# First phase of an encoder layer: summed rows, order of the next piece's sums, block-wise input turning, wider cumulation products

## The chip, the core and the metric

The kernel runs on one core of a Trainium2 chip. The metric is the device time of one execution in microseconds (us). Engines that appear below: TensorE (PE, with its weight loads PEld), VectorE (DVE), ScalarE (ACT), GpSimd (POOL) and SyncE (SP); POOL, SP and ACT issue DMA transfers.

## The reference

One layer of a hybrid encoder on x of 512 tokens by 2048, float32. A modulation vector made from the conditioning vector c shifts and scales the normalised input; one projection feeds attention (8 query heads, 2 key and value heads) and a gated delta net (8 heads, forward and backward), then come the output projection and a gated MLP.

```python
mod = silu(c) @ w_ada[l] + b_ada[l]              # 2048 x 12288
sh1, sc1, gt1, sh2, sc2, gt2 = jnp.split(mod, 6, axis=-1)
hn = rms_norm(h) * (1.0 + sc1) + sh1             # 512 x 2048
proj = hn @ w_in[l]
...
gc = jnp.cumsum(g.reshape(B, H, N, C), axis=-1)  # running sums of the log decay
```

The first phase of the kernel computes sh1, sc1 and hn, and the projections of both key and value heads of the attention, the first key and query heads of the delta net, and the 32 gate columns (ba).

## The kernel before

**Matrix products.** A float32 weight tile is split by ScalarE into w_hi (split, line 546, the copy in 551) and by VectorE into w_lo = raw - w_hi (low, 908, line 911); the activation is held as act_hi and act_lo. Three products (hi*hi, hi*lo, lo*hi; lines 1453 to 1455 in the first phase, 1359 to 1361 later) give one 128 x 128 x 512 step. A unit is eight weight tiles of 128 x 128 in one of two slots raw[0], raw[1]; SP loads unit u after lo_made counts u - 1.

**The first phase** runs over PIECES = (0,4), (4,8), (8,12), (12,14), (14,16): column tiles of 128 of the 2048 features. For piece j the modulation columns (shift and scale, 2 x 128 x the piece's width) are a sum over 16 row blocks k of w_ada. POOL loads all of them in order of j and k (line 491), into five slots for summed rows (DD, EG, CL, T, act) and two for turned rows (ka, va); it waits, in this order, until a slot's last reader is done.
- Summed rows: VectorE multiplies the block by cond[:, k] and adds it to an accumulator (first_add, 913, lines 924 and 927); accumulators alternate between ada_acc and PTb. Twelve of 16.
- Turned rows, TURNED_ROWS = (3, 7, 11, 15): TensorE multiplies the block by the column cond[:, k] (first_turned, 1416, line 1423), straight into the sum in PSUM.
- first_sums(j) (1408, line 1412) adds the accumulator's partitions on TensorE, first_columns(j) (929, lines 934 and 935, VectorE) adds the bias and writes mod, ScalarE writes act_hi and hn_tmp for each feature tile (lines 598 and 602), VectorE writes act_lo (normed, 953, line 957).
- TensorE multiplies the piece by the weights of three units (first_unit, 1442): units 3j to 3j+2 for full pieces; units 9 and 10 for (12,14), 10 and 11 for (14,16). ba_part (1459, line 1464) makes the gate columns.

The order of the work is written out by hand on each engine. TensorE, for a full piece:

```python
                for i in range(3):
                    first_unit(3 * j + i, k0, k1)
                    first_turned(j + 1, TURNED_ROWS[i])
                if j:
                    ba_part(*PIECES[j - 1])
                first_turned(j + 1, TURNED_ROWS[3])
                first_sums(j + 1)
```

VectorE runs all 12 summed rows of a piece, with the lows of the current units between them, then first_columns and normed, and only then the next piece's rows.

**Before the first piece** x (four blocks of 128 tokens, one DMA each, all counted on one semaphore) is squared, normalised by ScalarE (lines 576 to 584), turned by TensorE in 16 feature tiles of four blocks (line 1437) and copied to x_feat by ScalarE (line 590). TensorE starts on that behind all four turned rows of piece 0; ahead of these it turns the vector rows (line 1395) into col, once all small transfers have landed.

**After the phase** the weights of head 0 are multiplied (early, 1505) while the gates are worked out: 16 products of 8 columns make running sums within a block of 128 tokens (line 1527). The level masks are loaded as float32, cast by VectorE to bfloat16 (line 1027), and head 0 starts behind that cast.

## Time and profile before

| | us |
|---|---|
| median of 3 runs | 2695.82 |
| lowest, highest | 2693.03, 2696.62 |
| profiled execution | 2691.72 |
| its span | 2689.9 |

In the profiled execution PE is busy for 96% of the span, DVE for 52%, ACT for 38%, POOL for 8%. In 40 equal slices of the span (digits are tenths) the first two or three stand out:

```profile
PE   4889999999999989988999999999999999999997
DVE  3645666666666666445444444444444444444454
...
PEclk9889999999999989999999999999999999999998
DMA  8752544544544525432333333333333333333233
```

A slice is 67.2 us. PEclk is the granted clock of TensorE in tenths of full speed; DMA is the mean busy share of 16 transfer engines.

### The profile page before, as it was taken

The page shows a single profiled execution, that of the slowest core. Times are in us where ns is not written, and L with a number is a line of the kernel's source. Part 1 is how long each engine was busy: PE and PEld are TensorE (multiplying, and loading weights), DVE is VectorE, ACT ScalarE, POOL GpSimd, SP SyncE. Part 2 cuts the span into 40 slices and gives each one's busy share as a digit, 9 for nine tenths or more (in the row PEclk, how much of TensorE's full clock was granted, in tenths as well). Part 3 has the DMA queues.
Part 4 walks back from the last instruction along what each step waited for, and adds up shares of the span by engine and source line. Part 5 has one row for each costly group of instructions (what it writes and reads, how often), then busy time and mean ns, then how long its engine had stood idle before and what let it go on. Part 6 is the DMA issues. An engine that isn't in the chain of part 4 may idle for free.

```text
span 2689.9 us, 35982 instructions
## 1 busy us (share of the span) xinstructions
PE 2587.1 (96%) x12454; PEld 2126.7 (79%) x12454; DVE 1408.2 (52%) x1830; ACT 1029.2 (38%) x1438; POOL 214.2 (8%) x286
## 2 busy tenths in 40 slices
PE   4889999999999989988999999999999999999997
PEld 4777887888888868866888888888888888888885
DVE  3645666666666666445444444444444444444454
ACT  5224354354354353334443234442244432223334
POOL 2320211211211212100000000000000000000000
PEclk9889999999999989999999999999999999999998
DMA  8752544544544525432333333333333333333233
GB/s 290 274 171 68 154 123 125 156 120 129 151 118 131 152 86 153 139 88 71 94 95 91 96 101 100 94 92 96 101 94 100 94 88 96 104 101 94 87 92 126
DMA packets 431809, 318.46 MB, mean 118 GB/s; under 512 B 12902, under 2 KB 403857, under 8 KB 431249
## 3 DMA queue, kind: packets, MB, share of 16 engines
q1 hardware_dynamic: 401648, 212.19, 27.3%
q0 software_dynamic: 29184, 104.87, 12.1%
q10 hardware_dynamic: 929, 0.74, 0.1%
q8 instruction: 33, 0.54, 0.1%
q14 instruction: 15, 0.12, 0.0%
HBM read 313.56 MB, written 4.19 MB: 118 GB/s over the span
## 4 chain that ended last, share of the span: by engine, by line
PE 92%; DVE 3%; DMA 2%; ACT 1%; issue 1%; DVEq 0%; ACTq 0%; POOL 0%; POOLq 0%
PE pw L1359 23%; PE pw L1361 22%; PE pw L1360 22%; PE pw L1343 2%; PE pw L1345 2%; PE pw L1344 2%; PE pd L1626 2%; PE pd L1649 1%; PE pd L1662 1%; PE pd L1609 1%; DMA EG<-in_w_ada_dram 1%; PE pd L1669 1%; PE pd L1423 1%; DMA va<-in_w_ada_dram 1%; PE pd L1453 1%
## 5 line engine op out<-in xcount | busy, mean ns | idle before, releaser
L1359 PE MATMUL pw<-act_hi,w_hi 128*128 128x512 f32 x2016 | 813.5, 404 | 14.9 <-DVE act_lo L1254 8.7
L911 DVE TENSOR_TENSOR w_lo<-raw,w_hi 128x1024 fp32r<-128x1024 f32 x426 | 520.9, 1223 | 527.0 <-ACT w_hi L551 524.5
L1361 PE MATMUL pw<-act_hi,w_lo 128*128 128x512 f32 x2016 | 787.9, 391 | 0.0
L1360 PE MATMUL pw<-act_lo,w_hi 128*128 128x512 f32 x2016 | 786.2, 390 | 0.0
L551 ACT ACTIVATE w_hi<-raw 128x1024 fp32r<-128x1024 f32 x426 | 450.1, 1057 | 525.9 <-PE pw L1361 411.8
L1359 PEld LDWEIGHTS pw<-act_hi,w_hi 128*128 128x128 f32 x2016 | 379.6, 188 | 108.1 <-issue 24.9
L1361 PEld LDWEIGHTS pw<-act_hi,w_lo 128*128 128x128 f32 x2016 | 379.3, 188 | 81.5
L1360 PEld LDWEIGHTS pw<-act_lo,w_hi 128*128 128x128 f32 x2016 | 380.1, 189 | 80.4 <-issue 6.9
L1359 PE MATMUL pw<-mh_hi,w_hi 128*128 128x512 f32 x704 | 276.1, 392 | 1.6 <-DVE w_lo L911 1.6
L1361 PE MATMUL pw<-mh_hi,w_lo 128*128 128x512 f32 x704 | 274.2, 389 | 0.0
L1360 PE MATMUL pw<-mh_lo,w_hi 128*128 128x512 f32 x704 | 274.0, 389 | 0.0
L1279 DVE TENSOR_SCALAR cv<-gp,col 128x512 f32<-128x512 f32 x88 | 48.1, 547 | 298.4 <-ACT gp L847 298.4
L847 ACT ACTIVATE gp<-pw 128x512 f32<-128x512 f32 x88 | 52.7, 599 | 339.0 <-PE pw L1361 339.0
L1359 PEld LDWEIGHTS pw<-mh_hi,w_hi 128*128 128x128 f32 x704 | 132.2, 188 | 31.3 <-DVE w_lo L911 2.5
L946 DVE SCALAR_TENSOR_TENSOR ada_acc<-ada_w,cond,ada_acc 128x1024 f32<-128x1024 f32 x120 | 153.6, 1280 | 5.4 <-DMA ada_w<-in_w_ada_dram 3.8
L1361 PEld LDWEIGHTS pw<-mh_hi,w_lo 128*128 128x128 f32 x704 | 132.1, 188 | 27.8
L1360 PEld LDWEIGHTS pw<-mh_lo,w_hi 128*128 128x128 f32 x704 | 132.2, 188 | 26.9
L1283 DVE SCALAR_TENSOR_TENSOR cv<-gp,col,cv 128x512 f32<-128x512 f32 x176 | 132.4, 752 | 26.0 <-DVE cv L1283 5.2
L1343 PE MATMUL pw<-act_hi,w_hi 128*128 128x512 f32 x256 | 104.1, 407 | 10.0 <-DVE act_lo L1036 8.1
L1127 DVE SCALAR_TENSOR_TENSOR T<-pd,cst_sb,T 128x256 f32<-128x256 f32 x96 | 42.0, 480 | 127.7 <-PE pd L1662 127.7
L500 POOL DMA_DIRECT2D ada_w<-in_w_ada_dram x128 | 71.3, 557 | 411.1 <-DVE ada_acc L946 402.1
L1345 PE MATMUL pw<-act_hi,w_lo 128*128 128x512 f32 x256 | 100.5, 393 | 0.0
(280 smaller groups left out, 2682.4 us busy)
## 6 DMA issues: line engine op xcount, KB each, us to landing
raw<-in_w_up_dram SPq DMA_DIRECT2D x176, 512.0 KB, 3.9
ada_w<-in_w_ada_dram POOLq DMA_DIRECT2D x128, 512.0 KB, 4.4
raw<-in_w_in_dram SPq DMA_DIRECT2D x84, 512.0 KB, 3.9
raw<-in_w_down_dram SPq DMA_DIRECT2D x64, 384.0 KB, 3.4
raw<-in_w_down_dram SPq DMA_DIRECT2D x64, 320.0 KB, 3.1
raw<-in_w_out_dram SPq DMA_DIRECT2D x32, 512.0 KB, 4.4
DD<-in_w_ada_dram POOLq DMA_DIRECT2D x8, 512.0 KB, 8.2
mixed<-in_x_dram SPq DMA_DIRECT2D x4, 1024.0 KB, 13.4
```

The lines of the kernel that those rows point to most:

```text
L500: pool.dma_start(ada_w[k % 2][:], A["w_ada"][0, k * P:(k + 1) * P, bass.ds((4 + h) * ADA_W, ADA_W)]) \
L551: nc.scalar.activation(w_hi[slot][:], raw[slot][:], ACT.Copy).then_inc(hi_made.sem, 1)
L911: V.tensor_tensor(w_lo[slot][:], raw[slot][:], w_hi[slot][:].bitcast(F32), ALU.subtract).then_inc(lo_made.sem, 1)
L946: V.scalar_tensor_tensor(ada_acc[:], w, cond[:, k:k + 1], ada_acc[:], ALU.mult, ALU.add).then_inc(ada_step.sem, 1)
L1283: V.scalar_tensor_tensor(cv[:, part, :], gp[:, part, j:j + S], w[j], cv[:, part, :], ALU.mult, ALU.add) \
L1343: M(pw[slot][:], w_hi[slot][:, k, :], act_hi[:, t, :], start=k == 0, stop=False)
L1344: M(pw[slot][:], w_hi[slot][:, k, :], act_lo[:, t, :], start=False, stop=False)
L1345: ins = M(pw[slot][:], w_lo[slot][:, k, :], act_hi[:, t, :], start=False, stop=k == UK - 1)
L1359: M(bank, w_hi[slot][:, k, :], hi[:, k0 + k, :], start=first, stop=False)
L1360: M(bank, w_hi[slot][:, k, :], lo[:, k0 + k, :], start=False, stop=False)
L1361: ins = M(bank, w_lo[slot][:, k, :], hi[:, k0 + k, :], start=False, stop=last)
L1626: ins = TR(blk(pd[2 + d], b), T[:, d, b, :], ident)
```

## The change

- TURNED_ROWS has two rows, 5 and 11, in place of four: VectorE sums 14 row blocks of each piece.
- first_sums(j + 1) stands in the middle of the last unit of piece j, between its two halves; for piece 4 it stands ahead of a ba_part. VectorE adds the first two row blocks of piece j, then runs first_columns(j - 1), then goes on with a row block and an act_lo in turn (ahead). ScalarE's halves and splits are written out in an order of their own.
- Each block of x has its own semaphore. ScalarE squares and normalises a block as it lands; TensorE turns it (x_turn), four feature tiles to a bank; VectorE copies it to x_feat (x_block), between row blocks of piece 0. The turning of the vector rows and the gate row's product move behind it, to other banks.
- SP issues the first two units ahead of wba.
- The level masks come as bfloat16 bits in one transfer, issued by ScalarE's queue at the start; the casts go, and POOL waits for the transfer ahead of head 0.
- The running sums are made by 4 products of 32 columns.

```diff
--- before.py
+++ after.py
...
-TURNED_ROWS = (3, 7, 11, 15)
+TURNED_ROWS = (5, 11)
...
-    m = np.zeros((P, LEVELS, P), np.float32)
+    m = np.zeros((P, LEVELS, P), np.uint16)
     for n in range(LEVELS):
         b = 1 << n
-        m[:, n] = (p // (2 * b) == f // (2 * b)) & (p // b != f // b)
+        m[:, n] = np.where((p // (2 * b) == f // (2 * b)) & (p // b != f // b), 0x3F80, 0)
...
+        consts_in, rows_in, c_in = sem("consts_in"), sem("rows_in"), sem("c_in")
+        x_loaded = [sem(f"x_loaded{b}") for b in range(NB)]
         x2_in, stored, ba_in, small_in = [sem(f"x2_in{i}") for i in range(X_SLOTS)], sem("stored"), sem("ba_in"), sem("small_in")
-        lvl_in = [sem(f"lvl_in{i}") for i in range(2)]
+        lvl_in = sem("lvl_in")
...
-        x_squared, x_rstd = signal("x_squared", NB), signal("x_rstd", 2)
+        x_squared, x_rstd = signal("x_squared", NB), signal("x_rstd", 2 * NB)
...
             for b in range(NB):
-                sp.dma_start(x_in[:, b, :], A["x"][0, b * P:(b + 1) * P, :]).then_inc(x_loaded, 16)
+                sp.dma_start(x_in[:, b, :], A["x"][0, b * P:(b + 1) * P, :]).then_inc(x_loaded[b], 16)
             sp.dma_start(cst[:, C_FIRST:C_N], A["shape_constants"][:, C_FIRST:C_N]).then_inc(more_in, 16)
-            sp.dma_start(wba, w_in[:, COL_BA:COL_BA + 32].rearrange("(k p) n -> p k n", p=P)).then_inc(ba_in, 16)
...
-            for u in range(12):
+            first_unit(0)
+            first_unit(1)
+            sp.dma_start(wba, w_in[:, COL_BA:COL_BA + 32].rearrange("(k p) n -> p k n", p=P)).then_inc(ba_in, 16)
+            for u in range(2, 12):
                 first_unit(u)
...
+            pool.wait_ge(lvl_in, 16)
             head(0, first=True)
...
+            act.dma_start(lvl[:].rearrange("p l n -> p (l n)"), A["level_masks"].bitcast(BF16)).then_inc(lvl_in, 16)
+
             def split(q, slot, ahead=True):
 
...
             nc.scalar.activation(cond[:], pd[3][:, 0:KT], ACT.Silu).then_inc(cond_made.sem, 1)
             nc.scalar.preload_act_table_set(LOG_EXP)
-            act.wait_ge(*gate_row_sum.after(0))
-            nc.scalar.activation(gates[:, 0, :], pd[2][:, 0:16], ACT.Copy).then_inc(gates_made.sem, 1)
-            nc.scalar.activation(gates[:, 1, :], pd[2][:, 16:32], ACT.Exp).then_inc(gates_made.sem, 1)
...
             for b in range(NB):
+                act.wait_ge(x_loaded[b], 16)
                 if b:
                     act.wait_ge(*x_squared.after(0, b))
                 nc.scalar.activation(junk, x_in[:, b, :], ACT.Square, accum_out=nrm[:, 0, b:b + 1]).then_inc(x_squared.sem, 1)
-            act.wait_ge(*x_squared.after(0))
-            act.wait_ge(consts_in, 16)
-            nc.scalar.activation(nrm[:, 1, :], nrm[:, 0, :], ACT.Ln, scale=1.0 / DM, bias=eps1).then_inc(x_rstd.sem, 1)
-            act.wait_ge(*x_rstd.after(0, 1))
-            nc.scalar.activation(nrm[:, 2, :], nrm[:, 1, :], ACT.Exp, scale=-0.5).then_inc(x_rstd.sem, 1)
-            act.wait_ge(*x_rstd.after(0))
-            for b in range(NB):
+                act.wait_ge(*x_squared.after(0, b + 1))
+                if b == 0:
+                    act.wait_ge(consts_in, 16)
+                nc.scalar.activation(nrm[:, 1, b:b + 1], nrm[:, 0, b:b + 1], ACT.Ln, scale=1.0 / DM, bias=eps1).then_inc(x_rstd.sem, 1)
+                act.wait_ge(*x_rstd.after(0, 2 * b + 1))
+                nc.scalar.activation(nrm[:, 2, b:b + 1], nrm[:, 1, b:b + 1], ACT.Exp, scale=-0.5).then_inc(x_rstd.sem, 1)
+                act.wait_ge(*x_rstd.after(0, 2 * b + 2))
                 nc.scalar.activation(x_in[:, b, :], x_in[:, b, :], ACT.Identity, scale=nrm[:, 2, b:b + 1]) \
                     .then_inc(x_normed.sem, 1)
             split(0, 0, ahead=False)
             split(0, 1, ahead=False)
-            for m in range(KT):
-                act.wait_ge(*xt_sum.after(0, m + 1))
-                nc.scalar.activation(x_feat[:, m, :], pd[m % 4], ACT.Copy).then_inc(x_turned.sem, 1)
+            act.wait_ge(*gate_row_sum.after(0))
+            nc.scalar.activation(gates[:, 0, :], pd[4][:, 0:16], ACT.Copy).then_inc(gates_made.sem, 1)
+            nc.scalar.activation(gates[:, 1, :], pd[4][:, 16:32], ACT.Exp).then_inc(gates_made.sem, 1)
...
-            for j, (k0, k1) in enumerate(PIECES):
+
+            def first_split(u):
+
+                if u in (2, 5, 8, 10):
+                    act.wait_ge(q_in, 16 * ((2, 5, 8, 10).index(u) + 1))
+                split(u // 2, u % 2)
+
+            def first_halves(j):
+
                 act.wait_ge(*first_out.after(j))
-                for m in range(k0, k1):
+                for m in range(*PIECES[j]):
                     nc.scalar.activation(act_hi[:, m, :], x_feat[:, m, :], ACT.Identity, scale=mod[:, 16 + m:17 + m],
...
-                for u in ((2, 3, 4), (5, 6, 7), (8, 9, 10), (11,), (12,))[j]:
-                    if u in (2, 5, 8, 10):
-                        act.wait_ge(q_in, 16 * ((2, 5, 8, 10).index(u) + 1))
-                    split(u // 2, u % 2)
+
+            first_halves(0)
+            first_split(2)
+            first_split(3)
+            first_halves(1)
+            first_split(4)
+            first_split(5)
+            first_split(6)
+            first_halves(2)
+            first_split(7)
+            first_split(8)
+            first_split(9)
+            first_halves(3)
+            first_split(10)
+            first_split(11)
+            first_halves(4)
+            first_split(12)
...
-            for i, (c0, c1) in enumerate(LVL_COLS):
-                act.dma_start(lvl_f32[i], A["level_masks"][:, c0:c1]).then_inc(lvl_in[i], 16)
...
-            lows = ({12: 0, 14: 1}, {6: 2, 10: 3, 14: 4}, {6: 5, 10: 6, 14: 7}, {8: 8, 12: 9, 14: 10}, {12: 11})
-            for j, (k0, k1) in enumerate(PIECES):
-                for k in summed_rows:
+            def x_block(b):
+
+                for q in range(4):
+                    dve.wait_ge(*xt_sum.after(0, 4 * b + q + 1))
+                    V.tensor_copy(x_feat[:, 4 * q:4 * q + 4, b * P:(b + 1) * P], blocks(pd[q])).then_inc(x_turned.sem, 1)
+
+            for i, k in enumerate(summed_rows):
+                first_add(0, k)
+                if i in (2, 4, 6, 8):
+                    x_block((2, 4, 6, 8).index(i))
+                if i in (10, 11):
+                    low(0, i - 10)
+
+            def ahead(j, lows):
+
+                tiles = range(*PIECES[j - 1])
+                for i, k in enumerate(summed_rows):
                     first_add(j, k)
-                    if j == 0 and k == 6:
+                    if i == 0 and j == 1:
                         dve.wait_ge(*cols_sum.after(0))
-                        V.tensor_copy(col[:, 0:443], pd[0][:, 0:443]).then_inc(cols_made.sem, 1)
-                        V.tensor_copy(col[:, 443:V_N], pd[1][:, 0:V_N - 443]).then_inc(cols_made.sem, 1)
-                    if k in lows[j]:
-                        low(lows[j][k] // 2, lows[j][k] % 2)
-                    if j == 1 and k == 13:
+                        V.tensor_copy(col[:, 0:443], pw[0][:, 0:443]).then_inc(cols_made.sem, 1)
+                        V.tensor_copy(col[:, 443:V_N], pw[1][:, 0:V_N - 443]).then_inc(cols_made.sem, 1)
+                        dve.wait_ge(*cols_made.after(0))
+                    if i == 1:
+                        first_columns(j - 1)
+                        dve.wait_ge(*first_out.after(j - 1))
+                    if 2 <= i < 2 + len(tiles):
+                        normed(tiles[i - 2])
+                    if i == 6 and j == 1:
                         dve.wait_ge(*ba_split.after(0, 1))
                         V.tensor_tensor(wba_lo[:], wba, wba_hi[:].bitcast(F32), ALU.subtract).then_inc(ba_split.sem, 1)
-                dve.wait_ge(*cols_made.after(0))
-                first_columns(j)
-                dve.wait_ge(*first_out.after(j))
-                for m in range(k0, k1):
-                    normed(m)
+                    if i in lows:
+                        low(lows[i] // 2, lows[i] % 2)
+
+            ahead(1, {7: 2, 11: 3})
+            ahead(2, {5: 4, 8: 5, 12: 6})
+            ahead(3, {5: 7, 9: 8, 13: 9})
+            ahead(4, {5: 10})
+            low(5, 1)
+            last = len(PIECES) - 1
+            first_columns(last)
+            dve.wait_ge(*first_out.after(last))
+            for m in range(*PIECES[last]):
+                normed(m)
...
-            for i, (c0, c1) in enumerate(LVL_COLS):
-                dve.wait_ge(lvl_in[i], 16)
-                V.tensor_copy(lvl[:].rearrange("p l n -> p (l n)")[:, c0:c1], lvl_f32[i]).then_inc(lvl_made.sem, 1)
...
-            pe.wait_ge(rows_in, 16 * 10)
-            at_col = 0
-            for i, n in enumerate((115, 72, 128, 128, 96)):
-                bank, c0 = (0, at_col) if i < 4 else (1, at_col - 443)
...
-            ins.then_inc(cols_sum.sem, 1)
-            pe.wait_ge(small_in, 32)
-            M(pd[2][:, 0:32], ones[0:1, :], arow, start=True, stop=True).then_inc(gate_row_sum.sem, 1)
...
-            for k in TURNED_ROWS:
-                first_turned(0, k)
-            pe.wait_ge(*x_normed.after(0))
-            pe.wait_ge(*gates_made.after(0))
-            pe.wait_ge(*cols_made.after(0))
-            for m in range(KT):
-                if m >= 4:
-                    pe.wait_ge(*x_turned.after(0, m - 3))
-                for b in range(NB):
-                    ins = TR(pd[m % 4][:, b * P:(b + 1) * P], x_in[:, b, m * P:(m + 1) * P], ident)
-                ins.then_inc(xt_sum.sem, 1)
+
+            def x_turn(b):
+
+                pe.wait_ge(*x_normed.after(0, b + 1))
+                for q in range(4):
+                    if b:
+                        pe.wait_ge(*x_turned.after(0, 4 * (b - 1) + q + 1))
+                    for m in range(4):
+                        ins = TR(pd[q][:, m * P:(m + 1) * P], x_in[:, b, (4 * q + m) * P:(4 * q + m + 1) * P], ident)
+                    ins.then_inc(xt_sum.sem, 1)
+
+            x_turn(0)
+            x_turn(1)
+            first_turned(0, TURNED_ROWS[0])
+            x_turn(2)
+            x_turn(3)
+            pe.wait_ge(rows_in, 16 * 10)
...
+            pe.wait_ge(small_in, 32)
+            M(pd[4][:, 0:32], ones[0:1, :], arow, start=True, stop=True).then_inc(gate_row_sum.sem, 1)
+            first_turned(0, TURNED_ROWS[1])
             first_sums(0)
...
             for j in range(3):
                 k0, k1 = PIECES[j]
-                for i in range(3):
-                    first_unit(3 * j + i, k0, k1)
-                    first_turned(j + 1, TURNED_ROWS[i])
+                first_unit(3 * j, k0, k1)
+                first_turned(j + 1, TURNED_ROWS[0])
+                first_unit(3 * j + 1, k0, k1)
                 if j:
                     ba_part(*PIECES[j - 1])
-                first_turned(j + 1, TURNED_ROWS[3])
+                first_turned(j + 1, TURNED_ROWS[1])
+                first_unit(3 * j + 2, k0, k0 + 2, end=False)
                 first_sums(j + 1)
+                first_unit(3 * j + 2, k0 + 2, k1)
             first_unit(9, 12, 14)
             first_turned(4, TURNED_ROWS[0])
             first_unit(10, 12, 14, end=False)
             first_turned(4, TURNED_ROWS[1])
+            first_sums(4)
             ba_part(*PIECES[2])
-            first_turned(4, TURNED_ROWS[2])
-            first_turned(4, TURNED_ROWS[3])
-            first_sums(4)
             first_unit(10, 14, 16)
             first_unit(11, 14, 16)
             ba_part(12, 16)
...
             for i, c0 in enumerate((C_CUM, C_REST)):
-                for b in range(NB):
-                    for d in range(2):
-                        o = i * 64 + b * 16 + d * 8
-                        ins = M(pd[5][:, o:o + 8], cst[:, c0 + d * P:c0 + (d + 1) * P], gall[:, 1, b, d, :], start=True, stop=True)
+                for d in range(2):
+                    to = pd[5][:, i * 64:(i + 1) * 64].rearrange("p (b d h) -> p b d h", d=2, h=HEADS)[:, :, d, :]
+                    ins = M(to, cst[:, c0 + d * P:c0 + (d + 1) * P], gall[:, 1, :, d, :], start=True, stop=True)
...
-            pe.wait_ge(*lvl_made.after(0))
```

## Rows read from the trace of the kernel before

**Rows 1.** The page's first line: span of the profiled execution.

```profile
span 2689.9 us, 35982 instructions
```

**Rows 2.** Stretches of the first phase: busy time and instructions by engine, clock, DMA.

```profile
core 0: us, PE busy (x) PEld busy (x) DVE busy (x) ACT busy (x) POOL busy (x), PEclk, DMA share, GB/s
...
10.00:20.00 10.00, 0.00 (x0) 0.00 (x0) 3.32 (x3) 0.00 (x0) 2.44 (x4) 1.00 1.02 405
...
66.00:94.00 28.00, 26.61 (x143) 23.86 (x141) 18.50 (x16) 3.17 (x3) 11.53 (x16) 0.86 0.93 330
```

**Rows 3.** TensorE in order of time: start, duration, line, operand shapes, [idle before <-releaser].

```profile
44.18 3.57 PE L1423 MATMUL pd<-cond,va 128*128 128x1 f32 x16 [3.39 <-DMA va<-in_w_ada_dram]
...
47.61 9.44 PE L1437 MATMUL pd<-cst_sb,mixed 128*128 128x128 f32 x64
56.89 1.84 PE L1412 MATMUL pd<-cst_sb,ada_acc 128*128 128x1 f32 x16
...
61.66 0.77 PE L1453 MATMUL pw<-act_hi,w_hi 128*128 128x512 f32 x1 [2.92 <-DVE act_lo L957]
62.22 0.63 PE L1454 MATMUL pw<-act_lo,w_hi 128*128 128x512 f32 x1
62.65 0.63 PE L1455 MATMUL pw<-act_hi,w_lo 128*128 128x512 f32 x1
...
83.79 1.84 PE L1423 MATMUL pd<-cond,ka 128*128 128x1 f32 x16
86.91 3.57 PE L1423 MATMUL pd<-cond,va 128*128 128x1 f32 x16 [1.28 <-DMA va<-in_w_ada_dram]
90.34 3.55 PE L1412 MATMUL pd<-cst_sb,PTb 128*128 128x1 f32 x16
...
96.75 0.77 PE L1453 MATMUL pw<-act_hi,w_hi 128*128 128x512 f32 x1 [2.86 <-DVE act_lo L957]
...
129.38 0.77 PE L1453 MATMUL pw<-act_hi,w_hi 128*128 128x512 f32 x1 [2.86 <-DVE act_lo L957]
...
158.23 0.77 PE L1453 MATMUL pw<-act_hi,w_hi 128*128 128x512 f32 x1 [2.85 <-DVE act_lo L957]
...
180.75 0.79 PE L1453 MATMUL pd<-act_hi,w_hi 128*128 128x512 f32 x1 [2.76 <-DVE act_lo L957]
...
190.72 0.39 PE L1454 MATMUL pd<-act_lo,w_hi 128*128 128x512 f32 x1
190.95 0.39 PE L1455 MATMUL pd<-act_hi,w_lo 128*128 128x512 f32 x1
```

**Rows 4.** VectorE in order of time, the same columns, first phase.

```profile
25.80 1.28 DVE L927 SCALAR_TENSOR_TENSOR ada_acc<-T,cond,ada_acc 128x1024 f32<-128x1024 f32 x1 [6.38 <-DMA T<-in_w_ada_dram]
...
29.78 0.61 DVE L966 COPY col<-pd 128x443 f32<-128x443 f32 x1
...
45.10 1.28 DVE L927 SCALAR_TENSOR_TENSOR ada_acc<-DD,cond,ada_acc 128x1024 f32<-128x1024 f32 x1
46.48 1.28 DVE L927 SCALAR_TENSOR_TENSOR ada_acc<-EG,cond,ada_acc 128x1024 f32<-128x1024 f32 x1
48.01 1.23 DVE L911 TENSOR_TENSOR w_lo<-raw,w_hi 128x1024 fp32r<-128x1024 f32 x1 [0.24 <-ACT w_hi L551]
...
60.81 0.69 DVE L957 TENSOR_TENSOR act_lo<-tmp,act_hi 128x512 fp32r<-128x512 f32 x1 [1.75 <-ACT tmp L602]
...
133.94 0.75 DVE L927 SCALAR_TENSOR_TENSOR PTb<-CL,cond,PTb 128x512 f32<-128x512 f32 x1
```

**Rows 5.** ScalarE, groups by line and shape to 194 us: busy us, mean ns.

```profile
L584 ACT ACTIVATE mixed<-mixed,nrm 128x2048 f32<-128x2048 f32 x4 | 7.7, 1990 | 0.0
...
L576 ACT ACTIVATE PTb<-mixed 128x2048 f32<-128x2048 f32 x4 | 7.6, 1910 | 0.1
```

**Rows 6.** DMA issues, 2 to 190 us: size of one, median us to landing.

```profile
DD<-in_w_ada_dram POOLq DMA_DIRECT2D x8, 512.0 KB, 8.2
```

**Rows 7.** TensorE in order of time: the products of the running sums.

```profile
207.59 3.63 PE L1527 MATMUL pd<-gall,cst_sb 128*128 128x8 f32 x32
```

**Rows 8.** VectorE in order of time: the first cast of the masks.

```profile
238.11 0.42 DVE L1027 CAST lvl<-ktok 128x512 bf16<-128x512 f32 x1
```

14 lines of the change are left out of this document (7 added, 7 removed).

## Prediction

> **What bounds the kernel now.** I read the span first [rows 1], then the busy shares by stretch [rows 2], then TensorE's instructions in order of time [rows 3] and, for each hole in them, VectorE's [rows 4]. After 194 us TensorE has hardly a hole down to the end, and the change touches little there. Everything it touches lies in the first phase, up to the last matmul of the twelfth weight unit, which ends at about 191.2 us [rows 3]. That phase is a chain of five rounds. Each round makes a piece of the modulation vector from 16 row blocks of w_ada, turns it into a piece of the normalised activation, and multiplies. Rounds open at 61.66, 96.75, 129.38, 158.23 and 180.75 us [rows 3]: the time of one round is 35.1, 32.6, 28.9, 22.5 us and, for the last, 10.4 to unit 11's end. Every round opens after an idle of 2.8 to 2.9 us, ended by act_lo from VectorE, and its first matmuls are 0.43 us apart instead of the 0.23 of the later ones [rows 3]: a 512-column stream at 1.2 GHz, then at 2.4. The three units of a full round need only 72 x 0.228 = 16.4 us; the rest is row products and sums with one moving column, and holes.
>
> **Phase before the first matmul.** Now: the last row block (row 15, a turned one) is taken at 44.18; its products take 3.57; then 64 turns of x, 9.44; the sums, 1.84; then 2.9 us until act_lo is there: 61.66 [rows 3]. The change takes x out of this chain and puts two row blocks more on VectorE. VectorE's new list: 14 sums at a pitch of 1.39 (45.10 to 46.48 [rows 4]), 16 copies of 512 elements from PSUM at an estimated 0.6 (443 elements took 0.61 [rows 4]), 2 lows at 1.2. Rows arrive slowly while x loads, so I place row 4 at 25.8, where it is added now, and count from there: rows 4 to 15 are 10 sums = 13.9, blocks 1 to 3 of x are 12 copies = 7.2, lows 2.4, and 1.2 us waiting for block 3, whose last turns come late because TensorE turns at the lower level in short stretches. Sum: 50.5 us. ScalarE is ahead of that: 1.91 + 1.99 + 0.7 = 4.6 us per block of x [rows 5], four blocks 18.4; with the first landing at an estimated 10 (1 MB at about half of the 405 GB/s that all queues share [rows 2], from 2 us on, and the row blocks ahead of it) it is done at 28. The other blocks need another 8 us at least at that rate, so they land one by one, and the four separate semaphores do give ScalarE an earlier start. The sums then run after little work, 3.55 as at 90.34 and not 1.84 [rows 3], and the same 2.9 follow: **first matmul at 57.0, gain 4.7**. Bounds: 0 if the turned blocks of x hold VectorE up once each (4 x 1.2), 9 if VectorE never waits and the sums are fast.
>
> The transfer of the two units' weights now goes ahead of the small-row transfer of wba on SP's queue; wba must be in before ScalarE's first halves at about 54, behind which the rest of its list stands. It moves the same bytes, so I cost it at nothing; the late end is 3 us. The level masks move to ScalarE's queue at the start, half the bytes (0.23 MB, about 0.6 us of transfer at 405 GB/s [rows 2]); the casts are counted below.
>
> **The round boundaries.** Two of four turned rows go (their products cost 1.84 or 3.57 per block on TensorE [rows 3], and VectorE takes 1.39 each). The next piece's sums stand before the last half unit (12 matmuls, 2.75 us), which covers the 2.9 us of modulation, halves and low. Of the first boundary, 83.8 to 96.75, this leaves the sums: the unit list of a full round is 16.4 (units) + 2 x 1.7 (turned rows) + 1.8 (sums) = 21.6, and 24.4 with the wba products (12 x 0.23 = 2.8) from the second on.
> VectorE's list in a full round is 14 sums = 18.8, 4 act_lo at 0.6 to 0.7 [rows 4] = 2.6, 2 or 3 lows = 2.4 to 3.5, columns and small parts 1.4: 25.2 to 26. So **VectorE becomes as long as TensorE**, and paces. act_lo now comes every 1.39 + 0.69 = 2.08 us against 6 x 0.228 = 1.37 that TensorE needs per row block: 2 us lost in a unit that begins at speed, nothing in the first, which begins slowly anyway. Walking both lists through:
> - round 0: 25.2 us (now 35.1), the next sums waiting about 1 us for VectorE: gain 9.9
> - round 1: 26.6 (now 32.6), TensorE's list and 2.1 of late act_lo: gain 6.0
> - round 2: the next piece is half as wide, a sum costs 0.75 [rows 4] plus 0.11, VectorE 18; TensorE 16.4 + 1.6 + 0.9 + 2.8 = 22.0 with waits (now 28.9): gain 6.9
> - round 3: VectorE's 14 sums, 2 act_lo, 2 lows end about 142 if the round opens at 131, TensorE's next sums follow and the wba products cover the modulation: 15.0 (now 22.5): gain 7.5
> - last: 36 matmuls at 0.228 instead of a slow start: 8.3 (now 10.4): gain 2.1
> Together with 4.7: 37.1 us.
>
> **Two deductions.** At the first boundary TensorE waits 1 us in a stretch of one-column products; at 86.91 such a wait of 1.28 was followed by products of 3.57 and sums of 3.55 and ten matmuls at 0.43 [rows 3]. That is 1.7 + 2.0 = 3.7 us, and I take it once. Transfers: a full round moves 8.39 MB of w_ada and 3 units of 0.52, 9.96 MB. The first stretch kept 405 GB/s with the transfer share full, the first round 330 at 0.93 [rows 2], which is 355 at a full share; between them I take 374: 26.6 us, 1.4 more than round 0 allows, and nothing for round 1. Deducted: 5.1.
> The Trainium skill (DMA: Bandwidth & Descriptors, Where 436 GB/s comes from) puts HBM traffic of one core at about 358 GB/s, which speaks against a change that leans harder on the queues. The stretch at 405 GB/s shows more than that here. By that figure a full round could not be under 27.8 us, and rounds 0 and 1 would lose 2.6 and 1.2 instead of 1.4: a median of 2663.
>
> **After the phase.** Sixteen products of 8 columns (32 records, 3.63 us [rows 7]) become four of 32 columns: 8 records, 0.9 us if a record costs what it costs now, since the weight load of 128 columns is the same; TensorE works without holes there, so 2.7 less 0.1 for wider streams: 2.6. Bounds 1.5 to 2.7. The wait for the cast masks goes, but unit 18's low ends only as the first cast starts, at 238.11 [rows 8], and the first unit of the next head needs that low: the two casts, 0.42 [rows 8] and an estimated 0.3, are what goes: 0.7. Gain 3.3 together, kept to the end, as what follows is paced by TensorE.
>
> **Sum.** 37.1 - 5.1 + 3.3 = 35.3. The profiled execution took 2691.7 us (span 2689.9 [rows 1] and 1.8 around it), so 2656.4 for it. The median of the runs is 2695.8, 4.1 above it: **2660 us**.
>
> **Rivals.**
> - Transfers pace every round. Five slots serve 14 summed rows; a slot's circle is landing 8.2 [rows 6], the issue itself an estimated 0.7, and the sum 1.4, so five rows need 10.3 us and 14 need 28.9. With 330 GB/s a full round is 30.2 us (losses 5.0 and 3.6), and the narrow ones, whose packets are half as long, lose about 7 more. For it: VectorE already waits for row blocks now, and slots are unchanged. Against: landing takes that long only when seven blocks are asked for in one burst, as now at each round's start. Gain 37.1 - 16 + 3.3 = 24.4: 2671. Chance 0.22.
> - The sums come late at each boundary, because VectorE is the longer list, and TensorE falls to the lower level in them: 3.7 twice, 2.9 twice: 37.1 - 13.2 + 3.3 = 27.2: 2669. Chance 0.15.
> - The lists close better: x costs nothing and no clock is lost; 37.1 + 4 + 3.3 = 44.4: 2651. Chance 0.10.
> - Slower: TensorE's clock. Now the units run as solid blocks; with act_lo every 2.08 us against 1.37 of work and one-column products between, it could stay at 1.2 GHz through the units. All 288 matmuls at 0.43 cost 57 us more, the 48 wba products 10: 67, less 4 for the twenty or so that the forecast has slow already, less 35.3, is 28 slower: 2723. It decides from some 180 of the 288 (35.3 over 0.199) at the lower level. For it: every hole in the rounds was followed by some ten slow matmuls. Against: now a round that begins cold is fast after ten matmuls. Chance 0.02.
> - The sums ahead gain nothing, because VectorE, blocked on a landing row, holds back the lows that the current unit needs, as queued behind it: each round stays as it was. That is no change but for 3.3: within or just over the bound. Chance 0.01.
>
> **Numbers.** The forecast has 0.50. Most of what can be unlike is on the small-gain side, so the range goes from 2647 (the good case, less the 4 us between the forecast and the bound before the first matmul) to 2677 (the transfer case, wba late by 3, and a cold boundary). Outside it I leave some 0.15. A difference of 0.2%, 5.4 us, is what a measurement of this kernel can tell from none. Faster 0.97, same 0.01, slower 0.02.
>
> **What would show it.** First matmul near 57 and VectorE busy without holes from 26 to 50; copies to x_feat at 0.6; rounds opening near 83, 110, 132; no idle before a round's first matmul above 0.5 us; unit 11 done near 159; the products of the running sums in 0.9. Wrong if rounds are still 30 us with VectorE waiting for DMA (then the first rival), or if TensorE waits for the sums and the matmuls behind are 0.43 apart (the second). The gain would be larger if VectorE's list in round 0 ended before TensorE arrives.

## The result, and the profile after

The changed kernel takes **2657.23 us** (median of 4 runs, 2655.02 to 2658.15), the kernel before 2694.43 (2690.69 to 2696.62): a ratio of 0.9863, interval 0.9852 to 0.9875, so 37 us or 1.4% faster. The forecast was 2660. The profiled execution took 2658.15 us, with a span of 2656.5; the forecast for it was 2656.4.

The page after, 40 slices of 66.4 us; the first slice of VectorE has gone from 3 to 6 tenths and that of the transfers from 8 to 9:

```profile
span 2656.5 us, 35703 instructions
...
PE   4999999999999899979999999999999999999997
...
DVE  6736666666666655464444444444444444444454
...
PEclk7999999999999999999999999999999999999998
DMA  9933454454443535323333333333333323333333
```

TensorE of the changed kernel in order of time (start, duration, line, operands, [idle before <- what ended it]), with the row that opens each round:

```profile
50.36 3.58 PE L1442 MATMUL pd<-cst_sb,ada_acc 128*128 128x1 f32 x16 [8.89 <-DVE ada_acc L945]
56.76 0.77 PE L1498 MATMUL pw<-act_hi,w_hi 128*128 128x512 f32 x1 [2.82 <-DVE act_lo L975]
...
76.17 1.95 PE L1442 MATMUL pd<-cst_sb,PTb 128*128 128x1 f32 x16 [0.48 <-DVE PTb L945]
77.98 0.48 PE L1498 MATMUL pd<-act_hi,w_hi 128*128 128x512 f32 x1
...
81.42 0.47 PE L1498 MATMUL pw<-act_hi,w_hi 128*128 128x512 f32 x1 [0.43 <-DVE act_lo L975]
...
84.29 0.50 PE L1498 MATMUL pw<-act_hi,w_hi 128*128 128x512 f32 x1 [1.25 <-DVE act_lo L975]
...
109.06 0.47 PE L1498 MATMUL pw<-act_hi,w_hi 128*128 128x512 f32 x1
...
131.16 0.47 PE L1498 MATMUL pw<-act_hi,w_hi 128*128 128x512 f32 x1
...
145.31 1.86 PE L1442 MATMUL pd<-cst_sb,ada_acc 128*128 128x1 f32 x8 [3.97 <-DVE ada_acc L945]
147.04 0.61 PE L1509 MATMUL pd<-act_hi,wba_hi 128*32 128x512 f32 x1
...
152.02 0.39 PE L1498 MATMUL pd<-act_hi,w_hi 128*128 128x512 f32 x1
...
159.98 0.39 PE L1500 MATMUL pd<-act_hi,w_lo 128*128 128x512 f32 x1
```

Against [rows 3], the 2.8 us of idle that opened every round is left at the first only, and with it the 0.43 us pace of cold matmuls (TensorE at the lower of its two levels): the first sums are made in the middle of a unit (76.17), the unit's second half follows at once and at full pace (77.98), and act_lo is 0.43 us late. Unit 11 ends at 160.4 (159.98 and 0.39), where it ended at 191.3: 31.0 us. One boundary is still open: the fifth piece's sums wait 3.97 us (145.31), and the twelve ba products (for the gate columns) behind them take 5.0 us (147.04 to 152.02) instead of 2.8.

For a second measure I use the start of head 0, VectorE's copy to gcur, because the intervals of the ratios below are 5 to 9 us wide; before it lay at 238.71. It comes from one execution of each kernel, so it has a scatter of its own: six traces whose work is the same up to the first matmul (the changed kernel, e1, e2, e3 and both e4) have that matmul at 55.64 to 56.76 us. A difference of 1 us at head 0 tells nothing.

```profile
204.45 0.18 DVE L1091 COPY gcur<-gall 128x32 f32<-128x32 f32 x1
```

| kernel | median us | ratio to before, interval | head 0 at us |
|---|---|---|---|
| before | 2694.43 | 1 | 238.71 |
| changed | 2657.23 | 0.9863, 0.9852 to 0.9875 | 204.45 |
| sums behind the unit (e2) | 2664.67 | 0.9897, 0.9881 to 0.9914 | 210.97 |
| next transfers held (e3) | 2652.56 | 0.9853, 0.9836 to 0.9869 | 200.33 |
| only raw held (e4) | 2651.96 | 0.9850, 0.9834 to 0.9867 | 199.58 |
| only ada_w held (e4) | 2655.25 | 0.9864, 0.9848 to 0.9881 | 203.81 |
| four turned rows (e5) | 2672.41 | 0.9928, 0.9911 to 0.9944 | 219.87 |
| four turned, four slots (e7) | 2664.71 | 0.9900, 0.9883 to 0.9916 | 212.30 |
| x turned in one (e6) | 2654.71 | 0.9865, 0.9848 to 0.9881 | 203.15 |
| seven summed slots, held (e8) | 2651.80 | 0.9855, 0.9838 to 0.9871 | 196.19 |
| three turned at the start (e9) | 2652.64 | 0.9851, 0.9835 to 0.9868 | 199.25 |
| small cumulation products (e1) | 2661.42 | 0.9884, 0.9867 to 0.9901 | 206.23 |
| before, two turned rows (b1) | 2696.39 | 1.0015, 1.0005 to 1.0025 | 245.33 |
| before, four turned slots (b2) | 2694.29 | 1.0006, 0.9996 to 1.0015 | 239.56 |

Each ratio is taken to runs of the kernel before from the same session as the run (their medians lie between 2690.93 and 2694.43), so it is not the quotient of two medians of this table.

### The profile page after: what moved, and what is told of

It is laid out like the page before. It is cut to its first block, busy times and chain, and to the rows that moved or that the text cites. A ratio compares the mean times of both kernels' runs of the same rounds, so it can differ in the third digit from the quotient of the medians.

```text
span 2656.5 us, 35703 instructions
## 1 busy us (share of the span) xinstructions
PE 2560.8 (96%) x12302; PEld 2098.3 (79%) x12302; DVE 1425.2 (54%) x1854; ACT 1022.2 (38%) x1428; POOL 214.3 (8%) x286
## 3 DMA queue, kind: packets, MB, share of 16 engines
q1 hardware_dynamic: 401648, 212.19, 27.8%
## 4 chain that ended last, share of the span: by engine, by line
PE 92%; DVE 3%; DMA 1%; issue 1%; ACT 1%; POOL 0%; DVEq 0%; ACTq 0%; POOLq 0%
PE pw L1399 23%; PE pw L1401 23%; PE pw L1400 23%; PE pw L1383 2%; PE pw L1384 2%; PE pw L1385 2%; PE pd L1669 2%; PE pd L1692 2%; PE pd L1705 2%; PE pd L1652 1%; PE pd L1712 1%; DMA ka<-in_w_ada_dram 1%; DMA T<-in_w_ada_dram 1%; PE pd L1728 1%; PE pd L1723 1%
## 5 line engine op out<-in xcount | busy, mean ns | idle before, releaser
L1401 PEld LDWEIGHTS pw<-mh_hi,w_lo 128*128 128x128 f32 x704 | 132.1, 188 | 27.8
```

The lines of the kernel that those rows point to most:

```text
L1401: ins = M(bank, w_lo[slot][:, k, :], hi[:, k0 + k, :], start=False, stop=last)
```

## The experiments

### The place of the sums (e2)

```diff
-                first_unit(3 * j + 2, k0, k0 + 2, end=False)
+                first_unit(3 * j + 2, k0, k1)
                 first_sums(j + 1)
-                first_unit(3 * j + 2, k0 + 2, k1)
```

> The changed kernel with first_sums back behind the whole last unit of pieces 0 to 2. Theory (order on TensorE: the half unit covers the modulation step): each of three boundaries shows an idle of 2.8 to 2.9 us again and some ten matmuls at 0.43 us behind it, 2.0 more, so 14.7 slower, less the 2 us or so that the late act_lo and sums cost now: 12 to 13 us slower than the changed kernel, rounds of about 28, 31 and 27 us. Rival (transfers of row blocks pace the rounds): the idle moves only, at most 5 us slower.

Head 0 starts 6.5 us later than in the changed kernel, and the medians differ by 7.4 (9 by the ratios): less than expected. TensorE of e2 opens its rounds so:

```profile
82.68 0.47 PE L1498 MATMUL pw<-act_hi,w_hi 128*128 128x512 f32 x1 [2.76 <-DVE act_lo L975]
...
111.76 0.77 PE L1498 MATMUL pw<-act_hi,w_hi 128*128 128x512 f32 x1 [2.76 <-DVE act_lo L975]
```

Three boundaries have the old 2.76 us back, and behind each, at once or after three matmuls, 8 to 13 matmuls stand 0.43 us apart. What follows: the place of the sums is worth 6.5 of the 34 us at head 0. Part of the loss is given back. The waits for act_lo and for the first sums that TensorE has in rounds 0 and 1 of the changed kernel are gone, and the fifth piece's sums wait 1.21 us and not 3.97. The rows themselves are no earlier there: VectorE waits for the same two as long as in the changed kernel (2.35 and 1.23 us; 2.60 and 1.10). TensorE comes later to that wait, since 13 slow matmuls, 2.6 us, stand in the round. VectorE of e2:

```profile
148.80 0.75 DVE L945 SCALAR_TENSOR_TENSOR ada_acc<-EG,cond,ada_acc 128x512 f32<-128x512 f32 x1 [2.35 <-DMA EG<-in_w_ada_dram]
```

### The split of the rows alone, in the old order (b1), and slots in the old order (b2)

```diff
-TURNED_ROWS = (3, 7, 11, 15)
+TURNED_ROWS = (5, 11)
```

(and TensorE's calls for the two rows that are gone.)

> The kernel before with one thing of the change alone: two rows (5 and 11) turned by TensorE, fourteen summed by VectorE; the sums of the next piece stay where they were, behind the last unit. Nothing is left out. Theory: TensorE is freed of two turned rows a piece and POOL of its waits for TensorE (19.7 us in before), but VectorE now ends the piece's sums after TensorE's units, so each of the four boundaries opens with a wait for the sums: 2675 to 2683, 40 to 70 per cent of the whole gain. Rival (the place of the sums is what the change lives by, VectorE at 14 rows alone is too late): 2688 to 2694, no gain.

It is slower than before: the ratio is 1.0015 with an interval above one, 4 us, and head 0 comes 6.6 us later. Of these 6.6, 3.4 lie in the phase (unit 11 ends at 194.8 us, before at 191.3). The other 3.2 lie behind it and are TensorE's clock in this one execution: the products of the running sums take 4.67 us and not 3.63, and ten matmuls behind them are 0.43 us apart. Both theories had TensorE's relief right and overlooked what VectorE's old list does with two more rows. ScalarE, then VectorE of b1:

```profile
127.69 1.06 ACT L551 ACTIVATE w_hi<-raw 128x1024 fp32r<-128x1024 f32 x1 [14.26 <-PE pd L1455]
```
```profile
101.31 0.69 DVE L957 TENSOR_TENSOR act_lo<-tmp,act_hi 128x512 fp32r<-128x512 f32 x1 [0.72 <-ACT tmp L602]
...
128.78 1.23 DVE L911 TENSOR_TENSOR w_lo<-raw,w_hi 128x1024 fp32r<-128x1024 f32 x1 [6.06 <-ACT w_hi L551]
129.93 1.28 DVE L927 SCALAR_TENSOR_TENSOR ada_acc<-EG,cond,ada_acc 128x1024 f32<-128x1024 f32 x1
133.31 0.16 DVE L934 TENSOR_TENSOR mod<-pd,col 128x4 f32<-128x4 f32 x1 [2.11 <-PE pd L1412]
```

VectorE may not begin the next piece before the last act_lo (101.31), and between the four act_lo it waits for ScalarE (0.7 each). Near the end a low stands ahead of the last row: it waits 6.06 us for w_hi, which waits 14.26 us for TensorE to be done with the slot, and row 15, in no need of either, is queued behind. In the kernel before the same low waits too (1.28 us), but it is the last thing in the piece, since row 15 is TensorE's there. So two more rows on VectorE gain nothing in the old order; they pay only on top of another one.

```diff
-        turned_slots = [t[:].rearrange("p g n -> p (g n)") for t in (ka, va)]
+        turned_slots = [t[:].rearrange("p g n -> p (g n)") for t in (ka, va)] + [w[:] for w in ada_w]
```

(and n % 4 for n % 2, a wait for four slots in place of two, and the next stage's ada_w loads behind the phase.)

> The kernel before with four slots for the turned rows in place of two (the two buffers of ada_w are lent), its order of work untouched. Nothing is left out. POOL's waits for TensorE, 19.7 us in before, go. Theory (in the old order VectorE ends each piece late because it does the columns and lows of a piece before it may begin the next piece's rows, not because rows land late): within 3 us of before, 2689 to 2694. Rival (rows held up behind a turned row on POOL's queue cost the kernel before as they cost the run with four turned rows, where slots gave 7.7): 2681 to 2686.

Unchanged within its interval, as the theory wants, and POOL no longer waits for TensorE in this phase. But in the trace the zero is a sum:

```profile
65.31 0.77 PE L1455 MATMUL pw<-act_hi,w_hi 128*128 128x512 f32 x1 [2.92 <-DVE act_lo L959]
```

The first matmul comes 3.65 us later than before, and unit 11 still ends 0.7 earlier (190.6 us): the rounds are 4.4 us shorter. Behind the phase 1.6 go, 1.4 of them in seven matmuls at 0.43. So the slots gave something in the old order as well, about half of what the rival wanted. ScalarE's splits of the first two units wait 5.66 and 1.50 us for raw there, ahead of its copies of x (before: the second alone, 3.00); that the rows which POOL now asks for earlier held those weights up is argued, not shown.

### Four turned rows in the new order (e5, e7)

```diff
-TURNED_ROWS = (5, 11)
+TURNED_ROWS = (3, 7, 11, 15)
...
                 first_unit(3 * j + 1, k0, k1)
+                first_turned(j + 1, TURNED_ROWS[1])
                 if j:
                     ba_part(*PIECES[j - 1])
-                first_turned(j + 1, TURNED_ROWS[1])
+                first_turned(j + 1, TURNED_ROWS[2])
                 first_unit(3 * j + 2, k0, k0 + 2, end=False)
+                first_turned(j + 1, TURNED_ROWS[3])
                 first_sums(j + 1)
```

(The first and the fifth piece take their further turned rows directly ahead of the sums, and the last low of two rounds stands one or two rows earlier, since VectorE has twelve.)

> The changed kernel with four turned rows (3, 7, 11, 15) again, everything else kept. Theory (two lists): VectorE's list is shorter by 2.8 us in a full round, TensorE's longer by 3.4; the first matmul comes up to 2 us earlier, rounds 0 and 1 are 2 to 3.4 us longer, round 2 1.6 to 1.9 longer, round 3 shorter by the 1.7 that VectorE saves: together 3 to 6 us slower than the changed kernel. Rival (transfers pace the rounds, the bytes are the same): within 1 us.

Head 0 starts 15.4 us later than in the changed kernel, well beyond what was expected. The waits of POOL up to 175 us (in total, times, longest), then VectorE in order of time, both of e5:

```profile
POOL ka L492 <- PE pd L1453: 30.4, 7, 8.5
POOL va L492 <- PE pd L1453: 22.4, 7, 8.0
```
```profile
75.71 1.28 DVE L945 SCALAR_TENSOR_TENSOR PTb<-EG,cond,PTb 128x1024 f32<-128x1024 f32 x1 [5.72 <-DMA EG<-in_w_ada_dram]
```

POOL issues the rows in order. While it waits for TensorE to free ka or va (52.8 us altogether, none in the changed kernel), the summed rows behind are not asked for, and VectorE stands. In the changed kernel the slots of the two turned rows are free whenever POOL comes to them. That was a guess until the run that gives each turned row its own slot (the same slots as in b2, the same four rows):

> Four of the sixteen rows are turned by TensorE, as in the run with four turned rows, but each turned row of a piece has a slot of its own (the two buffers of ada_w are lent for it, and the two later loads that fill them are issued only when the phase has used its last row). Nothing is left out. Theory (POOL's queue is in order: in the run with four turned rows POOL waited 52.8 us for TensorE to free ka and va, and the rows behind came late to VectorE): POOL no longer waits for TensorE, VectorE's waits for landed rows fall from about 24 us to under 8, and the time is 2659 to 2664, that is 9 to 13 us below the run with two slots and 2 to 6 above the changed kernel. Rival (the two more turned rows cost this on TensorE itself, or the transfers pace the phase whatever the slots): 2669 to 2674.

Half of the loss goes (7.6 us at head 0, 7.7 by the medians), and POOL's waits for TensorE with it. The other half stays, and now it is TensorE's. VectorE, then TensorE of e7:

```profile
103.36 0.75 DVE L947 SCALAR_TENSOR_TENSOR PTb<-CL,cond,PTb 128x512 f32<-128x512 f32 x1
114.17 0.16 DVE L954 TENSOR_TENSOR mod<-pd,col 128x4 f32<-128x4 f32 x1 [10.07 <-PE pd L1444]
```
```profile
109.28 1.84 PE L1455 MATMUL pd<-cond,ada_w 128*128 128x1 f32 x16
110.98 3.16 PE L1444 MATMUL pd<-cst_sb,ada_acc 128*128 128x1 f32 x16
...
114.57 0.63 PE L1502 MATMUL pd<-act_lo,w_hi 128*128 128x512 f32 x1
115.00 0.63 PE L1503 MATMUL pd<-act_hi,w_lo 128*128 128x512 f32 x1
```

VectorE has its last row of the piece at 103 and waits 10 us; TensorE had no hole. Two more turned rows are 3.7 us of TensorE in a wide round and 1.9 in a narrow one, 11 in four rounds, of which TensorE's waits in the changed kernel cover a part, and the last turned row directly ahead of the sums makes a stretch of one-column products behind which the matmuls are 0.43 us apart. From 50 to 195 us the trace of e7 has 50 matmuls of 512 columns at that pace and the changed kernel's 17; at 0.2 us each that is 6.6 us. So the two rows moved to VectorE are worth 15 us once the order is new: about half on POOL's queue, half on TensorE, the greater part of that in its clock. The median of e7 is 7.5 us above the changed kernel's where I expected 2 to 6: the expectation left the clock out.

### The late rows of the fifth piece (e3, e4)

SP waits for VectorE's last row of the phase ahead of the raw loads of the next stage, and POOL ahead of its ada_w loads (both in e3, one each in the two others):

```diff
+            sp.wait_ge(first_step.sem, first_steps(len(PIECES) - 1, summed_rows[-1]))
             for t, c0 in ((2, COL_V), (3, COL_QA), (4, COL_Z)):
...
+            pool.wait_ge(first_step.sem, first_steps(len(PIECES) - 1, summed_rows[-1]))
             pool.wait_ge(*cols_made.after(0))
```

> The changed kernel; SP waits with the weights of unit 12 onwards, and GpSimd with the two prefetched blocks of ada_w, until VectorE has added the last row block of the first phase. Theory A (these transfers take bandwidth from the last four row blocks, for which VectorE waited 2.6 and 1.1 us): the last sum is made near 141 instead of 145.2, the sums on TensorE follow without the slow level, the twelfth unit ends near 155 and the time falls by 4 to 6 us. Rival (five slots and the order of the waits set when the last rows are asked for): the last sum stays at 145 and the time within 1 us of the changed kernel. If the held weights come too late, unit 12 opens with an idle and the time rises.

> The changed kernel with only the four raw loads of the next stage (unit 12 on, 512 bytes to a row) held back until the phase has used its last row; the two ada_w loads stay where they are. Nothing is left out. If the raw loads are what delayed the last rows of the fifth piece, this alone gives all of the 2.7 us that holding both gave: 2654.5. If it is ada_w, which lies behind those rows on the same queue, nothing: 2657. If it is their sum that takes the link, about half: 2656.

> The changed kernel with only POOL's two ada_w loads of the next stage held back until the phase has used its last row. Nothing is left out. Holding back the raw loads alone gave 2652.0, as much as both (2652.6). If the raw loads alone are the cause, this stays at 2656 to 2658. If any one of the two suffices to free the link, it gives 2652 to 2654.

With both waits, or with SP's alone, head 0 starts 4.1 and 4.9 us earlier, with POOL's alone 0.6, all of it ahead of the first matmul. In the changed kernel VectorE reads, first; then TensorE with raw held:

```profile
140.91 0.75 DVE L945 SCALAR_TENSOR_TENSOR ada_acc<-EG,cond,ada_acc 128x512 f32<-128x512 f32 x1 [2.60 <-DMA EG<-in_w_ada_dram]
142.77 0.75 DVE L945 SCALAR_TENSOR_TENSOR ada_acc<-CL,cond,ada_acc 128x512 f32<-128x512 f32 x1 [1.10 <-DMA CL<-in_w_ada_dram]
```
```profile
141.90 1.42 PE L1443 MATMUL pd<-cst_sb,ada_acc 128*128 128x1 f32 x8 [1.01 <-DVE ada_acc L946]
```

The DMA issues from 130 to 142 us (size, median us to landing), of the changed kernel and then with raw held, fit that: the first of SP's raw loads leaves at 135.11, in the middle of the last rows. In the queue line, that of SP's queue, the numbers are packets, MB and the share of 16 engines.

```profile
q1 hardware_dynamic: 1029, 0.52, 16.1%
...
EG<-in_w_ada_dram POOLq DMA_DIRECT2D x1, 256.0 KB, 6.1
CL<-in_w_ada_dram POOLq DMA_DIRECT2D x1, 256.0 KB, 6.7
```
```profile
EG<-in_w_ada_dram POOLq DMA_DIRECT2D x1, 256.0 KB, 3.7
CL<-in_w_ada_dram POOLq DMA_DIRECT2D x1, 256.0 KB, 3.2
```

Of the 4.9 us, 0.9 lie ahead of the first matmul, where the edit does nothing; 4.0 are the late rows and what the wait for them does to the clock. The slow level does not go altogether, as I had expected: six ba products are still 0.43 us apart with raw held, eleven in the changed kernel. Holding the raw loads costs nothing that the trace shows. The ratios alone would not tell these kernels from the changed one (their intervals overlap with its own); it is the rows' waits, gone with SP's wait and there with POOL's, that show the cause.

### Where the rows still set the pace (e8, e9)

e8 is e3 with two more slots:

```diff
-        summed_slots = [two(DD[:]), EGf, two(CL[:]), two(T[:]), act3[:, 0:2, :].rearrange("p t n -> p (t n)")]
+        summed_slots = [two(DD[:]), EGf, two(CL[:]), two(T[:]), act3[:, 0:2, :].rearrange("p t n -> p (t n)")] + [w[:] for w in ada_w]
```

> The changed kernel with the next stage's transfers held back until the phase has used its last row, and with seven slots for the summed rows in place of five. Nothing is left out. Theory (what remains of VectorE's waits for landed rows is a row issued late because its slot was not free): those waits, 7.6 us in the changed kernel's rounds, fall to under 2, and the time is 2649 to 2651, 2 to 3 us below the run that only holds the transfers back (2652.6). Rival (the link's rate paces these rows, so slots move nothing): 2652 to 2654.

In the trace the theory holds: from 32 us to the end of the phase VectorE's waits for rows add up to 0.3 us at most, the fifth piece's sums come at 139.90 after 0.45 us of idle, and head 0 starts at 196.19, 4.1 us earlier than in e3. The medians, 2651.80 and 2652.56, don't show it, and the four runs spread over 6.6 us (2648.66 to 2655.22). Whether the slots make the kernel faster stays open; that the rows are no longer late is shown.

e9 is the kernel with raw held, and a third turned row in the first piece alone:

```diff
-TURNED_ROWS = (5, 11)
+TURNED_ROWS = ((5, 8, 11), (5, 11), (5, 11), (5, 11), (5, 11))
```

> The kernel with the raw loads held back (2652.0 us), and with rows 5, 8 and 11 of the first piece turned by TensorE, thirteen summed; the other four pieces stay at two and fourteen. Nothing is left out. In the changed kernel TensorE stands idle for 8.9 us before the first sums, waiting for VectorE, so one more turned row (3.6 us at the lower clock) lies in that gap and takes one row of 1.3 us from VectorE. Theory (VectorE sets the first piece): the first sums and the first matmul come 1.3 us earlier, and where TensorE's extra work keeps its clock up the sums take 1.84 in place of 3.58, another 1.7: 2649.0 to 2650.7. Rival (the landing of the last rows sets the first piece): no change, 2652.

TensorE of e9:

```profile
48.39 3.57 PE L1443 MATMUL pd<-cst_sb,ada_acc 128*128 128x1 f32 x16 [4.18 <-DVE ada_acc L946]
54.78 0.76 PE L1500 MATMUL pw<-act_hi,w_hi 128*128 128x512 f32 x1 [2.82 <-DVE act_lo L976]
...
139.94 1.69 PE L1443 MATMUL pd<-cst_sb,ada_acc 128*128 128x1 f32 x8 [1.09 <-DVE ada_acc L946]
```

The first matmul comes at 54.78, 1.1 us earlier than with raw held alone (55.84) and 0.9 below the earliest of the six equal starts, much as a row of 1.3 us would have it. The lead does not shrink through the rounds: round 2 opens at 106.51 us and not at 108.56, and the fifth piece's sums start 1.96 us earlier (139.94 against 141.90). It goes at the last boundary. There the sums take 1.69 and not 1.42 us, and all twelve ba products are 0.43 us apart, where raw held has six; the stretch behind them opens at 146.60 against 147.18. By head 0 only 0.3 us are left, and the median shows none. So the theory was right in its first part, VectorE sets the first piece, and wrong in its second, the sums stayed cold (3.57). The rival was wrong, the rows of the first piece set nothing here. What took the lead back was TensorE's clock at the last boundary. The transfers did not: they ran at a full share from 60 to 100 us in e9 (371 and 372 GB/s) as in e8 (377 and 372), and in e8, with seven slots, VectorE waited for no row in that time.

### The block-wise turning of x (e6)

```diff
-            x_turn(0)
-            x_turn(1)
             first_turned(0, TURNED_ROWS[0])
-            x_turn(2)
-            x_turn(3)
...
             first_turned(0, TURNED_ROWS[1])
+            pe.wait_ge(*x_normed.after(0))
+            for m in range(KT):
+                if m >= 4:
+                    pe.wait_ge(*x_turned.after(0, m - 3))
+                for b in range(NB):
+                    ins = TR(pd[m % 4][:, b * P:(b + 1) * P], x_in[:, b, m * P:(m + 1) * P], ident)
+                ins.then_inc(xt_sum.sem, 1)
             first_sums(0)
```

(the copies to x_feat are ScalarE's again.)

> The changed kernel with x taken in one again: ScalarE starts on it when all four blocks are there and copies it to x_feat, TensorE turns it behind both turned rows, VectorE has no copies. Theory: what cost time was that turning stood behind the last row block; here it stands beside the last sums on VectorE. x is normalised by 39 us, turned 43 to 53, the sums follow at full speed: first matmul near 57.5, within 1 us of the changed kernel's 56.8. Rival (the block-wise work is what gained the 4.9 us of the start): first matmul back at 61.7, 5 us slower.

The first matmul is at 55.66 and head 0 starts 1.3 us earlier than in the changed kernel, which is within the scatter of equal starts (55.64 to 56.76). VectorE, free of its copies, has its last row done at 47.7 us there (50.3 in the changed kernel), and TensorE turns x until 50.7; the sums, directly behind the turning, start 0.3 us later and run at 1.84 and not at 3.58. Turning x block by block is no part of the gain. In both forms it starts before VectorE's last rows and no longer behind the last row of all. That this place gains the 4.9 us of the start is what is left over; no run puts it back.

### The cumulation products (e1)

> The changed kernel with the sixteen-by-two cumulation products of 8 columns of the kernel before in place of the four of 32 columns. Nothing is left out. Theory (they lie on the path from the gates to the first head): 2.6 to 2.7 us slower than the changed kernel, 2659.9. Rival (the path into head 0 is set by VectorE's low halves and the products are hidden): same as the changed kernel, 2657.2.

TensorE of e1, and of the changed kernel:

```profile
175.70 3.63 PE L1572 MATMUL pd<-gall,cst_sb 128*128 128x8 f32 x32
```
```profile
176.62 0.97 PE L1571 MATMUL pd<-gall,cst_sb 128*128 128x32 f32 x8
```

2.66 us of difference; the products begin 0.9 us earlier in e1 and head 0 1.8 us later, which adds up to 2.7: the products are on the path. The medians are 4.2 apart, and the intervals of the ratios hold 2.7.

## Why the prediction was right, and where it was not

Step by step, the first column from the prediction:

| step | forecast us | measured us |
|---|---|---|
| first matmul | 57.0 | 56.76 |
| round 0 | 25.2 | 24.7 |
| round 1 | 26.6 | 27.6 |
| round 2 | 22.0 | 22.1 |
| round 3 | 15.0 | 20.9 |
| last, to unit 11 | 8.3 | 8.4 |
| cold boundary and transfers | 5.1 | in the rounds |
| behind the phase | 3.3 | 3.3 |

The forecast gain was 35.3 us and the measured one is 37, but one round in five was wrong by 5.9 us and the sum hides it. (Unit 11 of the kernel before ends at 191.3 us by [rows 3]; the prediction reads 191.2.)

- **Before the first matmul** the chain was right: VectorE busy from 27 on, copies of x at 0.62 us (four in 2.48), sums cold at 3.58, then 2.82 until act_lo. Two sizes in it were off and cancel: row 4 was added at 27.3 us and not at 25.8, and the last block of x held VectorE up for 0.16 us and not 1.2. The credit I gave to four separate landings of x was not needed for it, as e6 shows.
- **Rounds 0 to 2** hold to within 1.0 us. act_lo came late by 0.43 us at the end of round 0 and by 1.25 and 0.61 us in round 1, the 2 us forecast.
- **Round 3 is the step that failed.** I had VectorE end its rows at about 142; it ended at 145.2, as two rows landed late behind SP's transfers for the next stage, which I had left out of the sum. The wait of 3.97 and the cold products behind it (sums 1.86 instead of 0.95, ba 5.0 instead of 2.8) are 7.1 us, where the forecast had nothing but a term of 5.1 for other places. Without the transfers the same wait is 1.0 (e4).
- **The two deductions** were 5.1 us, and 5.9 went astray in round 3: the sum came out right because the cold boundary, which I put in round 0, happened, at another place and larger. In round 0 the sums waited 0.48 and stayed at full pace. That is luck in the sum, not insight. The mechanism was not wrong for round 0 either: other executions show it there, after the same wait. TensorE with raw held:

```profile
76.08 2.25 PE L1443 MATMUL pd<-cst_sb,PTb 128*128 128x1 f32 x16 [0.48 <-DVE PTb L946]
...
78.77 0.63 PE L1500 MATMUL pd<-act_lo,w_hi 128*128 128x512 f32 x1
79.19 0.63 PE L1501 MATMUL pd<-act_hi,w_lo 128*128 128x512 f32 x1
```

Fourteen matmuls are slow behind it, and round 2 still opens earlier than in the changed kernel (108.56 against 109.06): in that stretch VectorE sets the pace, and the slow matmuls fill waits for act_lo. So the 3.7 us that I took for a cold first boundary would have been too much even where it happens.
- **Transfers.** I took 374 GB/s for rounds 0 and 1. The stretches of the changed kernel, with the columns of [rows 2]:

```profile
60.00:80.00 20.00, 19.52 (x110) 16.63 (x110) 17.80 (x19) 3.74 (x6) 10.05 (x14) 1.00 1.04 374
80.00:100.00 20.00, 17.57 (x83) 12.55 (x81) 18.02 (x18) 7.36 (x9) 7.95 (x11) 1.00 1.03 375
```

That is the figure, but the 1.4 us that I deducted by it did not come: round 0 took 24.7 us and not 26.6. The figure also lies above the 358 GB/s of the Trainium skill (DMA: Bandwidth & Descriptors, Where 436 GB/s comes from), by which a full round is, as an estimate, 27.8 us at least; rounds 0 and 1 took 24.7 and 27.6. The rival in which the transfers pace every round did not come. A part of its mechanism is there: with five slots VectorE waits 7.6 us for rows in the rounds of the changed kernel, 3.7 of them for the two rows beside SP's loads, and with seven slots and the loads held it waits for none (e8). The clock stayed at the higher level through both stretches, so the slower rival had nothing to stand on; with raw held the same stretches have 0.93 and 0.89, far from its condition too.
- **The sums** coming late and cold, the second rival, happened at one boundary of four.
- **What I credited wrongly.** I argued the two fewer turned rows as TensorE's time and the place of the sums as what hides the modulation. Both are real (about 8 and 6.5 us). Missing was POOL's queue (7.6 us, from e5 and e7). What remains goes to the new order of the lists: with four turned rows and the sums in the unit (e5) head 0 is already 19 us ahead of before, 3.8 of it at the first matmul and some 3.3 from the products and casts behind the phase, while two turned rows in the old order (b1) are 7 behind. The other 12 are shared by the place of the sums and VectorE's list, in which the next piece's rows no longer stand behind act_lo; no run has that list without the rest, so its share is not shown.
- **To the end.** 34.3 us at head 0 ended as 33.4 in the span. The difference is TensorE's clock. A stretch of the changed kernel, then the same with raw held:

```profile
1040.00:1060.00 20.00, 18.13 (x86) 15.10 (x86) 8.65 (x13) 8.58 (x15) 6.14 (x9) 0.91 0.62 183
```
```profile
1040.00:1060.00 20.00, 20.00 (x108) 17.00 (x107) 7.67 (x10) 8.88 (x15) 6.67 (x9) 1.00 0.67 192
```

The hole of 1.9 us is the same in both, but in the changed kernel eight matmuls behind it are slow (PEclk 0.91) and 1.6 us went; with raw held the lead at head 0, 4.9 us, ends as 6.3. In the kernel before the same hole, at 1077.00 us, has no slow matmul behind it. From head 0 to the end of the span the fourteen traces take 2449.0 to 2452.9 us, so up to 4 us of difference between single executions come on top of any edit here.
- **The median.** I set it 4 us above the profiled execution, as it was before. Now it is 0.9 below. The forecast of the profiled execution was 1.8 too low and that of the median 2.8 too high.

## What to carry to other kernels

When engines hand work round in a loop, write down for each in-order queue what stands behind every instruction that can wait: here a low ahead of a row, a load into a slot that TensorE frees ahead of loads for VectorE, and next-stage loads that need no hurry each cost 4 to 8 us. Shift work between engines only after that; the same shift lost 4 us of the median in the old order and won 15 in the new one. And put a reduction with a long tail in the middle of the work that is to hide the tail, not behind it. The changed kernel with SP's next-stage loads held until the phase is over has the lowest ratio, 0.9850 (2651.96 us); with POOL's held too, with seven slots (e8) or with a third turned row at the start (e9) the ratio is the same within the intervals.
